# The last hybrid layer's products in one span of 512 tokens, and grid and window attention without filler between values and scores

## What is computed

```
# first block, layer 1: neighbourhood ("grid") attention, 16 heads of 64, queries are the latents alone
s_loc = q_row . k_band * scale + bias, masked      # 8 rows of 16 columns around the query
s_ctx = q_row . k_ctx * scale
o = softmax([s_loc, s_ctx]) @ [v_band, v_ctx];  y = o @ w_o
# second block, both layers
u = rms_norm(h, g);  q_r,k_r,v_r,g_r,q_a,k_a,v_a,gate_r,gate_a = split(u @ w_in)
y_r = (retention(q_r, k_r, v_r) * silu(g_r)) @ w_ret_o
y_a = window_attention(q_a, k_a, v_a, sink) @ w_att_o      # local: 128 to either side, and the meta tokens
mix = (sigmoid(gate_r) * y_r + sigmoid(gate_a) * y_a) @ w_mix_o
h = h + rms_norm(mix, g2);  u = rms_norm(h, g3)
h = h + rms_norm(square(relu(u @ w_ff1)) @ w_ff2, g4)
return h[:, 16:]                                    # the meta tokens are dropped
```

## Time and profile before

| | |
|---|---|
| median of 3 runs | 3798.76 us (3796.55 to 3801.59) |
| profiled execution | 3793.54 us, span 3791.6 us, mean granted TensorE clock 0.989 |
| PE busy | 3655.6 us, 96% |
| PEld busy | 3311.4 us, 87% |
| DVE busy | 1902.9 us, 50% |
| ACT busy | 1373.7 us, 36% |
| POOL busy | 462.8 us, 12% |
| PE in the chain that ended last | 90% |
| DMA, mean | 81 GB/s |

### The profile page before, as it was taken

One profiled execution on the slowest core, in us unless ns is written; L12 is line 12 of the kernel. 1 busy time (PEld: TensorE's weight loads), 2 busy tenths in 40 slices (PEclk: granted clock), 3 DMA queues, 4 the chain that ended last, 5 costly groups with the idle time before them and its releaser, 6 DMA issues.

```text
span 3791.6 us, 63596 instructions
## 1 busy us (share of the span) xinstructions
PE 3655.6 (96%) x26658; PEld 3311.4 (87%) x26658; DVE 1902.9 (50%) x3372; ACT 1373.7 (36%) x2699; POOL 462.8 (12%) x571
## 2 busy tenths in 40 slices
PE   8999999999999999999999999999998999999998
PEld 7777778888888887888899889999998988999998
DVE  4544556555544556544565654434445556443444
ACT  3445444122234444323422452442232235234232
POOL 1222211000012332000110100210012110011001
PEclk9999999999999999999999999999999999999999
DMA  5111221333322112222311112222221111222222
GB/s 189 67 64 50 69 86 64 128 123 117 122 78 67 62 49 67 87 97 97 111 51 45 46 65 87 73 95 90 90 84 34 51 56 54 95 81 90 91 94 73
DMA packets 88267, 307.03 MB, mean 81 GB/s; under 512 B 10016, under 2 KB 13216, under 8 KB 87728
## 3 DMA queue, kind: packets, MB, share of 16 engines
q1 hardware_dynamic: 85184, 293.25, 22.9%
q0 software_dynamic: 2800, 9.73, 0.8%
HBM read 300.84 MB, written 2.10 MB: 80 GB/s over the span
## 4 chain that ended last, share of the span: by engine, by line
PE 90%; DVE 4%; ACT 3%; POOL 1%; issue 1%; DMA 0%; SPq 0%; POOLq 0%; DVEq 0%; ACTq 0%
PE bank L581 66%; PE bank L643 6%; PE bank L612 2%; PE bank L1101 2%; PE bank L887 2%; PE bank L926 1%; PE bank L1087 1%; PE bank L832 1%; PE bank L954 1%; PE bank L979 1%; DVE weight_lo L1888 1%; PE bank L966 1%; PE bank L1197 1%; PE bank L1225 1%; PE bank L1210 1%
## 5 line engine op out<-in xcount | busy, mean ns | idle before, releaser
L1888 DVE TENSOR_TENSOR weight_lo<-weight_raw,weight_hi 128x1024 fp32r<-128x1024 f32 (+1 forms) x464 | 560.3, 1210 | 425.5 <-ACT weight_hi L1293 424.8
L1293 ACT ACTIVATE weight_hi<-weight_raw 128x1024 fp32r<-128x1024 f32 (+1 forms) x464 | 476.5, 1031 | 581.9 <-PE bank L581 371.4
L581 PE MATMUL bank<-u_hi,weight_hi 128*128 128x256 f32 (+1 forms) x2112 | 610.3, 289 | 2.4 <-DVE weight_lo L1888 2.3
L581 PE MATMUL bank<-u_lo,weight_hi 128*128 128x256 f32 (+1 forms) x2112 | 597.9, 283 | 0.0
L581 PE MATMUL bank<-u_hi,weight_lo 128*128 128x256 f32 (+1 forms) x2112 | 597.4, 283 | 0.0
L581 PE MATMUL bank<-h_hi,weight_hi 128*128 128x512 f32 (+1 forms) x1328 | 484.2, 365 | 13.8 <-DVE h_lo L2323 9.6
L581 PE MATMUL bank<-h_lo,weight_hi 128*128 128x512 f32 (+1 forms) x1328 | 466.6, 351 | 0.0
L581 PE MATMUL bank<-h_hi,weight_lo 128*128 128x512 f32 (+1 forms) x1328 | 466.3, 351 | 0.0
L581 PEld LDWEIGHTS bank<-u_hi,weight_hi 128*128 128x128 f32 x2112 | 398.4, 189 | 25.9 <-issue 20.7
L581 PEld LDWEIGHTS bank<-u_hi,weight_lo 128*128 128x128 f32 x2112 | 398.3, 189 | 0.0
L581 PEld LDWEIGHTS bank<-u_lo,weight_hi 128*128 128x128 f32 x2112 | 397.2, 188 | 0.2
(11 more groups left out here) (288 smaller groups left out, 7377.0 us busy)
## 6 DMA issues: line engine op xcount, KB each, us to landing
weight_raw<-in_w_mlp SPq DMA_DIRECT2D x128, 512.0 KB, 3.3
weight_raw<-in_w_ff SPq DMA_DIRECT2D x128, 512.0 KB, 3.3
weight_raw<-in_w_in SPq DMA_DIRECT2D x92, 512.0 KB, 3.3
weight_raw<-in_w_mod SPq DMA_DIRECT2D x80, 512.0 KB, 4.4
weight_raw<-in_a_w_qkv SPq DMA_DIRECT2D x24, 512.0 KB, 4.1
weight_raw<-in_b_w_qkv SPq DMA_DIRECT2D x24, 512.0 KB, 3.3
first_weight<-in_w_mod SPq DMA_DIRECT2D x16, 512.0 KB, 15.5
weight_raw<-in_w_ret_o SPq DMA_DIRECT2D x16, 512.0 KB, 3.3
```

Of the source, the lines that this page charges most:

```text
L581: m = e.matmul(view[:, 0:hi - lo], a[:, k, :], b[:, k0 + k, lo:hi], start=(k == 0 and i == 0), stop=(k == kt - 1 and i == 2))
L1293: e.activation(whi[s % N_SPLIT][:, 0:kt, :], raw[n % N_RAW][:, 0:kt, :], ACT.Copy).then_inc(*tick("act_split", ("hi", n)))
L1888: e.tensor_tensor(wlo[s][:, 0:kt, :], raw[n % N_RAW][:, 0:kt, :], whi[s][:, 0:kt, :].bitcast(F32), ALU.subtract).then_inc(*tick("dve_split ...
```

## The change

**Hybrid layer 1 in one span.** `WHOLE` is one span from 16 to 528, and `wide(layer)` gives it for layer 1. The query products, the retention gate, both gates, both branch outputs, five of eight mixo products and all MLP products but the three at either turn use it. Keys, the values and the products at the turns keep their spans. Evacuations on DVE and ACT are made once for 512 columns where they were made twice for 256; those that announce halves signal both.

**Packed rows.** Layer 1 gets tiles of its own with rows of 512 tokens: late_u for the input of the MLP, late_ret for the gated retention output and the mix, late_hidden for the MLP's inner part. `Latents` shifts the column numbers by 16. The input of w_in (u) keeps its rows of 528. mix_out_T (MO) moves to the place of retention_out_T in both layers.

**Joined values and scores.** `sweep` gets `joined`: the third `fill()` of a unit is left out but for the last unit. `near_units` and the window units of both layers set it; the fill's calls go from 3n+1 to 2n+2, so that each hands out more. Differential attention (`diff_units`) stays as it was.

```
+class Latents:
+    def __init__(self, ap):
+        self.ap = ap
+    def __getitem__(self, key):
+        part, k, cols = key
+        hi = N_HYB if cols.stop is None else cols.stop
+        return self.ap[part, k, cols.start - N_META:hi - N_META]
...
-def sweep(n, stages, fill, tail=()):
+def sweep(n, stages, fill, tail=(), joined=False):
...
         values(i)
-        fill()
+        if not joined or i + 1 == n:
+            fill()
...
-        MO = sb("mix_out_T", [P, KT, N_HYB], F32, o_h + KT * HYB)
+        MO = sb("mix_out_T", [P, KT, N_HYB], F32, o_r)
...
+        def latents(name, at_):
+            return [Latents(sb(f"{name}_{n}", [P, KT, N_LAT], F32R, at_ + i * KT * HYB)) for i, n in enumerate(("hi", "lo"))]
+
+        FF = [(U_HI, U_LO), latents("late_u", o_h)]
+        RET = [(OR_HI, OR_LO), latents("late_ret", o_z)]
+        FF_HID = [HYB_HID, latents("late_hidden", o_z)]
...
+        WHOLE = Tokens((N_META, N_HYB))
...
+        def wide(layer):
+
+            return HYBRID if layer == 0 else WHOLE
...
-                    fill = Fill(3 * n + 1, heads_cost(layer) + cost,
+                    fill = Fill((3 - layer) * n + 1 + layer, heads_cost(layer) + cost,
...
-                    yield from product_T(("rg", layer, m_), (w_in, 16 + m_), U_HI, U_LO, tok, ready)
+                    yield from product_T(("rg", layer, m_), (w_in, 16 + m_), U_HI, U_LO, wide(layer), ready)
...
-                        x, of = (AQ[:, i, :], tok) if i < 4 else (AK, HYBRID)
+                        x, of = (AQ[:, i, :], wide(layer)) if i < 4 else (AK, HYBRID)
...
-                fill = Fill(3 * len(units) + 1, 7 * product_cost(tok) + 3.0, win_project(1, 2, 3),
+                fill = Fill(2 * len(units) + 2, 7 * product_cost(wide(layer)) + 3.0, win_project(1, 2, 3),
...
-                for stage in sweep(len(units), (score, nothing, turn_weights, values, nothing, nothing), fill):
+                for stage in sweep(len(units), (score, nothing, turn_weights, values, nothing, nothing), fill, joined=True):
...
-                        run(product_T(("gate", layer, m_, part), (w_in, gate), U_HI, U_LO, tok, ready))
-                        run(product_T(("branch", layer, m_, part), wo, xh, xl, tok,
+                        run(product_T(("gate", layer, m_, part), (w_in, gate), U_HI, U_LO, wide(layer), ready))
+                        run(product_T(("branch", layer, m_, part), wo, xh, xl, wide(layer),
...
-                    run(product_T(("mixo", layer, m_), (f"w_mix_o{layer}", m_), OR_HI, OR_LO, tok, mixed))
+                    run(product_T(("mixo", layer, m_), (f"w_mix_o{layer}", m_), *RET[layer], wide(layer), mixed))
...
-                return mlp(name, U_HI, U_LO, HYB_HID, tok, tok, f"w_ff1_{layer}", f"w_ff2_{layer}",
+                return mlp(name, *FF[layer], FF_HID[layer], wide(layer), tok, f"w_ff1_{layer}", f"w_ff2_{layer}",
```

More of the change, by code:

```diff
@@ L457, in kept, with halves_of @@
             return HYBRID if layer == 0 else LATE
+        def wide(layer):
+            return HYBRID if layer == 0 else WHOLE
+        def halves_of(layer, span):
+            return (span,) if layer == 0 else (0, 1)
         def edge(layer):
@@ L521, in attention_groups @@
                     out = KT * product_cost(q_tokens(layer), 6)
-                    fill = Fill(3 * n + 1, out + cost, splits(), itertools.islice(side, 1),
+                    fill = Fill((3 - layer) * n + 1 + layer, out + cost, splits(), itertools.islice(side, 1),
                                 beside(output(), side, out / 5))
@@ L1672, in sigmoid @@
                     def sigmoid():
-                        for span, (lo, hi) in enumerate(tok.spans):
+                        for span, (lo, hi) in enumerate(wide(layer).spans):
                             e.wait_ge(*at("rgt", layer, m_, span))
@@ L1676, in sigmoid @@
                                 *tick("act_proj", ("rsig", layer, m_, span)))
-                    yield from later(product_T((w_in, 16 + m_), tok), 2, behind)
+                    yield from later(product_T((w_in, 16 + m_), wide(layer)), 2 - layer, behind)
                     behind.append(sigmoid)
@@ L1773, in turn_out @@
                         *tick("act_attn", ("free", "o", 2, layer, i)))
-                for stage in sweep(len(units), (score, expo, turn_weights, nothing, turn_out, nothing), fill):
+                for stage in sweep(len(units), (score, expo, turn_weights, nothing, turn_out, nothing), fill, joined=True):
                     stage()
@@ L2482, in evacuate @@
                             *tick("dve_mix", ("rgt", layer, m_, span), ("free", *job)))
-                    yield from later(product_T((w_in, 16 + m_), tok, evacuate), 5, behind)
+                    yield from later(product_T((w_in, 16 + m_), wide(layer), evacuate), 5 - 2 * layer, behind)
                     behind.append(gated)
@@ L2637, in expo @@
                             *tick("dve_attn", ("n", 2, layer, i, s)))
-                for stage in sweep(len(units), (score, expo, nothing, nothing, nothing, nothing), fill):
+                for stage in sweep(len(units), (score, expo, nothing, nothing, nothing, nothing), fill, joined=True):
                     stage()
@@ L2929, in gate_retention @@
                 def gate_retention(m_):
-                    for lo, hi in tok.spans:
+                    for lo, hi in wide(layer).spans:
                         yield from cost_T(hi - lo)
@@ L2988, in score @@
                             *tick("pool_attn", ("sink", layer, i, s)))
-                for stage in sweep(len(units), (score, nothing, nothing, nothing, nothing, nothing), fill):
+                for stage in sweep(len(units), (score, nothing, nothing, nothing, nothing, nothing), fill, joined=True):
                     stage()
```

102 lines of the change are left out of this document (53 added, 49 removed).

## The result

The changed kernel takes 3763.66 us (median of 4 runs, 3761.84 to 3766.15) where the kernel before takes 3797.66 in the same series: a ratio of 0.991, 95% interval 0.9898 to 0.9921, 34.0 us less. The prediction had 3760 and 38.5 us less. The profiled executions differ by 30.2 us (spans 3791.6 and 3761.4).

What follows compares the result with a forecast made beforehand. The prediction took PE's stream, busy 96% of the span, as the bound. Wide span 24.7, stage starts 3.0, join 7.8 and unit waits 3.0 sum to 38.5 us off 3798.76, so about 3760 us, range 3748 to 3776.

Steps and rivals of the forecast that it cites:

- the likeliest case: Whole kernel: the forecast's own case, 3750 to 3769 us, chance 0.78.
- B: Grid and window units: 41 fewer filler blocks ahead of scores, 0.19 us each, 7.8 us gained.
- C: Waits inside the units: larger filler portions cover more of PE's waits, 3.0 us gained, ends -4 to 7.
- The signal that I named: Window units in the profile after: idle time ahead of transposes and values below 15.1 us together.
- the second rival: Transposes in most units: DVE's filler work makes PE wait, the join gives its gain back, 3771 us; chance 0.12.
- A: Layer 1 products in one span of 512: 103 products save 0.24 us each, 24.7 us, ends 18.0 to 25.7.
- D: Starts of w2 and the first mixo product: waits at k 7 go, 1.4 + 1.55 = 3.0 us gained.
- I take rows 5, since their rows of 768 are no whole multiple of 512 either, and since at 256 columns u isn't slower than anything else: 28 gates and queries reading u: priced like the first block's w1 at 512 columns, 5.44 us per product.
- the bad end: 28 products reading u: if each costs no less than two halves, 6.7 us come off the gain.
- all of it lies on PE's own stream, and nothing hides it: All 103 products given one span: their whole 24.7 us shortens PE's stream and so the kernel.
- That the wide span saves little: Merged spans: a whole costs two halves, 5.68 us per product, time 3785.0; chance 0.07 up to a quarter gain.
- Slower: All 36 window units wait 2.06 us at a transposition that comes too early, 74 us, time 3837; chance 0.03.

Runs made afterwards that it cites:

- experiment 5: Kernel before with only the joined values and scores; layer 1 keeps spans of 256 and rows of 528, mix_out_T at its new place: 3787.21 us, ratio 0.9972.
- experiment 4: Kernel before with the join and packed rows, but spans of 256 in hybrid layer 1: 3791.49 us, ratio 0.998.
- experiment 2: Changed kernel without packed rows: layer 1's mix and MLP read tiles with rows of 528 again, spans stay 512 wide: 3771.46 us, ratio 0.9931.
- experiment 6: Changed kernel without the join: wide span and packed rows alone, filler in three portions again: 3780.20 us, ratio 0.9951.
- experiment 3: Changed kernel with packed tiles moved, late_u by 64 bytes, late_ret by 128, late_hidden by 32: 3771.50 us, ratio 0.9933.
- Experiment 8: Changed kernel with the mix stage's third weight split ahead of the window halves on ACT and DVE, both hybrid layers: 3759.81 us, ratio 0.99.
- experiment 9: Changed kernel with u in rows of 576, latents at column 64, so rows start at multiples of 256 bytes: 3767.67 us, ratio 0.9919.

## Why the prediction was right, and where it was off

The forecast of the gain was 4.5 us too large by the medians; the time lay inside the range, and the sign and the likeliest case were right. By parts (experiment 5 for the join, changed kernel less experiment 5 for the rest):

**The join (B and C)** was to bring 7.8 + 3.0 = 10.8 us; it brought 11.3 by the medians and 4.1 + 3.3 + 3.1 = 10.5 by stages. A block between 12 matmuls of values and scores took 1.71 us in before: 0.81 for the values, 6 x 0.118 for the filler, and 0.19 left, the price of the earlier trace rows. There are 12 + 14 + 13 = 39 blocks of filler fewer between first scores and last values of the three places, so 7.4 us are B and some 3 are left over, the size of C. But they aren't what C was made of. The signal that I named was idle time ahead of transposes and values below 15.1 us, and it failed: by the view of the earlier trace rows it is 16.1 in 13 places ahead of the transposes alone:

```profile
its engine sat idle before it (us, times) until:
  DVE scratch L2669: 16.1, 13
```

The sign, and the 19.7 us from which C was sized, rest on a misread view: it adds the idle time of PE's weight loads to that of its matmuls. What PE's matmuls alone waited for at transposes and rotations in the whole program (us in total, times, the longest), before and after:

```profile
PE bank L1210 <- DVE scratch L2636: 5.5, 6, 1.9
PE bank L1048 <- ACT win_q L1724: 4.6, 7, 1.0
```

```profile
PE bank L1239 <- DVE scratch L2669: 7.0, 6, 1.9
PE bank L1077 <- ACT win_q L1753: 3.8, 5, 1.2
```

Ahead of the values it was 0.3 us before and 0.7 after, not the 5.0 that the prediction took. So 10.4 us of 19.7 were there to be gained, and 11.5 are there after the change: the join shortened no idle time on balance, and that C's 3 us were met is luck. The transposes wait 1.5 us longer, which fits the second rival (DVE's filler work ahead of the normalized weights), at 1.5 of the 10.8 us that it needed; no run changes DVE's order alone. In window layer 0 the gain beyond B is in the time from transposes to what follows them (14.9 us before, 13.7 with the join); only 0.5 of it is idle time ahead of the values, in gaps that are mostly too short for the view above, and what the rest is stays open. The one unit of layer 1 with an empty portion waits 0.7 us for the copy, near the forecast 1 us.

**The wide span (A and D)** was to bring 27.7 us. It brought 23.1 by the medians (3787.2 - 3764.1, taken on two chips) and 20.7 by the stages:

| | forecast | stages |
|---|---|---|
| mixo, w1, w2: 63 products x 0.24, and D | 18.1 | 17.9 |
| first to last attention output product: 14 gates, 7 retention and 8 half-deep products | 6.0 | 3.7 |
| 4 queries, 8 retention gates: 7 in the window units, 5 ahead of them | 2.9 | 0.4 (0.1 and 0.2) |
| first three products of the mix stage | 0.7 | -1.3 |

The first line is right to 0.2, D included: the waits of the earlier trace rows fell under the wider cover as worked out. The Trainium skill's fixed 2.5 ns ("TensorE: Matmul & The Clock Gate", section "Wait — 56ns, not 53.3ns?") is not what these matmuls show: a merged pair gives back 10 ns, and for the 6.2 us of that rule the 17.7 us that the stages leave for A without D are nearly three times as much.

The second line is the step "I take rows 5, since their rows of 768 are no whole multiple of 512 either, and since at 256 columns u isn't slower than anything else". Rows 5 were aligned, at 12 x 256 bytes; I counted tokens where bytes matter. And 256 columns say nothing on 512: experiment 4 shows that there the unaligned rows are the faster ones. A gate cost 5.57, between the two ends that the prediction gave (5.44 and 5.68), so the step cost 28 x 0.13 = 3.6 us of the 6.7 of the bad end. The prediction gave the eight half-deep products, whose rows of 528 tokens it didn't name, the full gain as well; they lost some 0.5 us (8 x 12 x 5 ns). In this line it is 14 x 0.13 + 0.5 = 2.3 us, which is what is missing. For the packed tiles the choice was right, and experiment 2 prices it.

The third line is the step "all of it lies on PE's own stream, and nothing hides it". In the window units PE's stream isn't all. Their seven products gained 0.11 us each by their pace from u, 0.8 in all; but with the same filler in coarser pieces one portion between transposes and values fell empty, and the time from transposes to what follows grew from 12.2 us in experiment 5 to 13.5. Of the five products ahead of the units, at 0.55 us by their pace, the first rotation took back 0.3, since it waits for a copy of 512 columns and no longer of 256. Without the join the window units became 2.8 us longer than before (experiment 6). That is most of why the two parts aren't additive: 11.3 + 18.4 = 29.7 us apart, 34 together; the window units make 3.0 of the 4.3 us.

The fourth line is a wait that I hadn't looked for. From the last values on, ACT and DVE have a chain of fixed length: a table load and sigmoid, the retention's high halves, the window's, the third weight. The first matmul that needs this weight starts 13.58 us behind the last values before, and 13.44 after. Before, PE only just outlasted the chain: it waited 0.11 us there, its second product kept step with ret_lo for four k (0.6 us each and not 0.36), and six matmuls of filler, 0.7 us, stood behind the last values, which the change has moved ahead of them. So a faster stream could gain no more than 0.2 of the 0.7 us here and waited for the rest; the clock, which fell to half behind the wait, cost 1.5 more (19.07 us without it in experiments 2 and 3, 20.63 with it). Experiment 8 takes the wait and the clock back. The prediction listed what is late next for the waits that it removed, but not for a stage that showed almost none.

**Rivals.** That the wide span saves little: a pace of 0.2267 against 0.237 us settles it. That the join gives its gain back: at most 1.5 of 10.8 us. Slower: 6 of the 36 window units made PE wait at their transposes, 7.0 us in all, not 36 of them.

## What to carry to other kernels

When two spans are merged, check where each row of the moving operand starts in bytes, and pack or pad the tile along with it: here that was 7 to 8 us, a third of the wide span's gain, and packing without merging was a loss of 4. When work is used as filler between dependent steps, its piece must stay small against the number of places to fill, or the places be made fewer; the join and the wide span were worth more together than apart. Before speeding up a stream, look for the chains on other engines that it just outlasts; a wait of 0.1 us can mark one. Before sizing a gain from idle time, see which engine's idle time a view adds up.

## What the runs showed of the hardware

- fp32r matmuls with a weight load each, 512 columns: 226.7 ns start to start where each row of the operand starts at a multiple of 256 bytes, 228.9 at 64 bytes off, 232 at 128 off, 233.3 at 32 off (experiment 3), 231.7 on average with rows of 2112 bytes (experiment 2). At 256 columns: 120.0 with aligned rows (experiment 4), 118.3 with rows of 2112 bytes. Why the sign turns isn't known.
- Behind 1.9 to 2.0 us in which PE stood still, the clock fell to 1.2 GHz for 3.4 us in both traces of the changed kernel and in experiments 6 and 9 (20.59 to 20.63 us from the last values to the first attention output product), and not in experiments 2 and 3, which stood still for 1.82 us (19.06 and 19.08 us). What decides it stays open. The Trainium skill ("TensorE: Matmul & The Clock Gate", section "Wait — 56ns, not 53.3ns?") gives columns over 1.2 GHz for that level, 426.7 ns at 512 columns, and the trace agrees with 0.43 us.
